# Expert stages: when each half of the next gate and up weights is loaded

## What is computed

```python
def block(args):
    tids, e, w = args
    xb = x_pad[tids]
    hdn = jax.nn.silu(xb @ w1[e]) * (xb @ w3[e])
    return (hdn @ w2[e]) * w[:, None].astype(xb.dtype)
```

## Time and profile before

| what | us |
|---|---|
| median of 3 runs | 3187.47 |
| lowest and highest | 3185.77 to 3190.87 |
| profiled execution, its own time | 3187.16 |
| its span, first to last instruction | 3185.40 |
| busy TensorE | 3063.2 |
| busy VectorE | 2140.7 |
| busy ScalarE | 1584.9 |
| busy GpSimd | 400.5 |

### The profile page before, as it was taken

How to read it: one execution, slowest core, us unless ns; L and a number is a source line. 1 busy time by engine, 2 the same in 40 slices (tenths; PEclk the granted TensorE clock), 3 DMA queues, 4 the chain that set the end, 5 groups by cost and what they waited for, 6 DMA issues and landing times.

```text
span 3185.4 us, 39317 instructions
## 1 busy us (share of the span) xinstructions
PE 3063.2 (96%) x14891; PEld 2373.3 (75%) x14891; DVE 2140.7 (67%) x2334; ACT 1584.9 (50%) x1905; POOL 400.5 (13%) x275
## 2 busy tenths in 40 slices
PE   8999899999999999999999989988999999999998
PEld 7668677777758867677776757877888888788887
DVE  3475788888863375888888865564476646767662
ACT  3573577777753271777777753442322223622211
POOL 0001222222220002222222240010000000000000
PEclk9999899999999998999999999999999999999999
DMA  7303699999972124899998963220223222232322
GB/s 271 113 1 126 261 362 359 349 363 356 353 273 100 37 77 169 327 357 351 344 364 342 357 200 93 53 53 1 93 80 106 93 106 93 86 113 80 106 93 79
DMA packets 174737, 600.47 MB, mean 189 GB/s; under 512 B 25538, under 2 KB 74866, under 8 KB 125204
## 3 DMA queue, kind: packets, MB, share of 16 engines
q1 hardware_dynamic: 140432, 541.22, 46.4%
q0 software_dynamic: 23680, 52.61, 4.6%
q10 hardware_dynamic: 10499, 4.91, 0.6%
HBM read 582.01 MB, written 48.23 MB: 198 GB/s over the span
## 4 chain that ended last, share of the span: by engine, by line
PE 84%; DMA 6%; DVE 4%; ACT 3%; issue 2%; POOL 1%; DVEq 0%; SPq 0%; POOLq 0%; ACTq 0%
PE bank L1948 21%; PE bank L1950 21%; PE bank L1949 21%; PE bank L1960 3%; DMA ring<-w_gate 2%; PE bank L2617 2%; PE bank L2012 1%; PE bank L2013 1%; PE bank L2341 1%; PE bank L1955 1%; DMA expert_rows<-lnp 1%; PE bank L1956 1%; PE bank L2306 1%; PE bank L2112 1%; PE bank L2378 1%
## 5 line engine op out<-in xcount | busy, mean ns | idle before, releaser
L1949 PE MATMUL bank<-ring_rounded,big_rounded 128*96 128x512 f32 (+1 forms) x1768 | 696.0, 394 | 0.0
L3363 DVE TENSOR_TENSOR ring_rounded<-ring,big_rounded 128x2048 fp32r<-128x2048 f32 x252 | 567.2, 2287 | 38.6 <-ACT big_rounded L1389 37.1
L1389 ACT ACTIVATE big_rounded<-ring 128x2048 fp32r<-128x2048 f32 x252 | 478.3, 1918 | 63.3 <-DMA ring<-w_up 53.4
L2916 DVE TENSOR_TENSOR ring_rounded<-ring,ring_rounded 128x2048 fp32r<-128x2048 f32 (+2 forms) x118 | 260.3, 2245 | 334.4 <-ACT ring_rounded L1146 334.1
L1146 ACT ACTIVATE ring_rounded<-ring 128x2048 fp32r<-128x2048 f32 (+2 forms) x124 | 226.7, 1877 | 376.0 <-DMA ring<-ffn_w_down 151.1
L1948 PE MATMUL bank<-big_rounded 128*96 128x512 f32 x992 | 394.7, 398 | 0.4 <-DVE ring_rounded L3363 0.4
L3363 DVE TENSOR_TENSOR ring_rounded<-ring,ring_rounded 128x2048 fp32r<-128x2048 f32 x128 | 292.7, 2288 | 151.3 <-ACT ring_rounded L1389 150.7
L1950 PE MATMUL bank<-big_rounded,XH_rounded 128*96 128x512 f32 x992 | 392.1, 395 | 0.0
L1949 PEld LDWEIGHTS bank<-ring_rounded,big_rounded 128*96 128x96 f32 (+1 forms) x1768 | 294.6, 167 | 109.3
L1389 ACT ACTIVATE ring_rounded<-ring 128x2048 fp32r<-128x2048 f32 x128 | 245.0, 1916 | 223.2 <-DMA ring<-w_gate 222.9
L1948 PE MATMUL bank<-ring_rounded,big_rounded 128*96 128x512 f32 (+1 forms) x776 | 312.3, 403 | 10.7 <-issue 5.1
(11 more groups left out here) (484 smaller groups left out, 5052.9 us busy)
## 6 DMA issues: line engine op xcount, KB each, us to landing
ring<-w_up SPq DMA_DIRECT2D x128, 1024.0 KB, 7.9
ring<-w_down SPq DMA_DIRECT2D x128, 1024.0 KB, 7.9
ring<-w_gate SPq DMA_DIRECT2D x128, 1024.0 KB, 5.5
ring<-ffn_w_up SPq DMA_DIRECT2D x44, 1024.0 KB, 7.5
ring<-ret_gdn_w_in SPq DMA_DIRECT2D x8, 2048.0 KB, 12.8
ring<-ffn_w_down SPq DMA_DIRECT2D x8, 2048.0 KB, 7.8
expert_rows<-lnp POOLq DMA_DIRECT2D x1, 12288.0 KB, 41.9
ring<-odd_w_qkv SPq DMA_DIRECT2D x6, 2048.0 KB, 7.9
```

The lines of the kernel that those rows point to most:

```text
L1389: act.activation(one_pass(expert_hi(j)), expert_raw(j), ACT.Copy).then_inc(signal("half_rounded").sem, 1)
L1949: pe.matmul(dst, x_hi, y_lo, start=False, stop=False)
L2916: dve.tensor_tensor(one_pass(w), w, parts(hi(c)[:, ks, :]), ALU.subtract).then_inc(split[c.pair], 1)
L3363: dve.tensor_tensor(one_pass(expert_raw(j)), expert_raw(j), parts(expert_hi(j)), ALU.subtract).then_inc(signal("half_split").sem, 1)
```

## The change

There is one new signal, `half_used`, in place of `down_half`. TensorE increments it after the fourth of the eight steps of gate and of up, and after the first half of the down products, three times for each expert. SP waits for it before the first half of gate and of up, and issues that half alone; the second half is issued behind `full[2]` or `full[3]`, as before. In the first expert of a layer the increments come after the first four of the products with the remainders. The first down half of the last expert gets the same treatment. `halves_used` counts the increments. A helper with no caller, `keep_busy`, is removed.

```diff
@@ load_experts and beside it
+        def halves_used(l, e):
+
+            return 3 * EXPERTS * l + 1 if isinstance(e, int) and e == 0 else e * 3 + 3 * EXPERTS * l
+
@@
                 def next_gate_up(e):
 
-                    for b, js in ((2, GATE), (3, UP)):
+                    for i, (b, js) in enumerate(((2, GATE), (3, UP))):
+                        sp.wait_ge(signal("half_used").sem, halves_used(l, e) + i)
+                        expert_half(e + 1, js[0])
                         sp.wait_ge(full[b], e + (base[b] + 1))
-                        for j in js:
-                            expert_half(e + 1, j)
+                        expert_half(e + 1, js[1])
 
                 def next_down(e):
 
-                    sp.wait_ge(signal("down_half").sem, e + EXPERTS * l)
+                    sp.wait_ge(signal("half_used").sem, halves_used(l, e) + 2)
                     expert_half(e, DOWN[0])
@@
-                sp.wait_ge(full[2], base[2] + EXPERTS)
                 w = a["w_down"][l][EXPERTS - 1].rearrange("(h p k) n -> h p k n", p=P, h=2)
                 for j in DOWN:
+                    if j == DOWN[0]:
+                        sp.wait_ge(signal("half_used").sem, halves_used(l, EXPERTS - 1))
+                    else:
+                        sp.wait_ge(full[2], base[2] + EXPERTS)
                     sp.dma_start(last_down(expert_raw, j), w[j % 2]).then_inc(half_loaded[j - 4], 16)
@@ up_first
                                 ins = remainder(psum[b][0:CAP, :], M["XET"][:, half, 4 * i + kk, :], expert_raw(j)[:, kk, :], 4 * i + kk == KD - 1)
+                            if i == 0:
+                                ins.then_inc(signal("half_used").sem, 1)
                         ins.then_inc(full[b], 1)
@@ up
                                           expert_hi(j)[:, kk % 4, :], expert_raw(j)[:, kk % 4, :], kk == 0, kk == KD - 1)
+                            if kk == 3:
+                                ins.then_inc(signal("half_used").sem, 1)
                         ins.then_inc(full[b], 1)
@@ down
                         if j == DOWN[0]:
-                            ins.then_inc(signal("down_half").sem, 1)
+                            ins.then_inc(signal("half_used").sem, 1)
```

More of the change, by code:

```diff
@@ L2207, in turn_qk @@
                     ins.then_inc(full[v.bank], 1)
-            def keep_busy(v, n):
-                pe.matmul(ps(v)[:, 0:n], ident, const[:, 0:n], start=True, stop=True)
             def windows():
```

## The result

The changed kernel takes 3163.57 us (median of 6, 3161.89 to 3169.86) against 3185.93 us for the kernel before, measured beside it. The ratio is 0.9929, with a 95% interval of 0.9913 to 0.9944: 22.4 us, 0.7% faster. Later, in another comparison of the same two kernels, it was 3164.99 and 0.9929 (0.9911 to 0.9947).

The account below looks back on a forecast made before the run. TensorE, 96% busy, was taken as the bound, losing time when the first gate half lands late. Terms 18 + 1.0 + 2.5 = 21.5, say 22 us, gave 3187.2 - 22 = 3165 us, range 3159 to 3176 (8 in 10).

Parts of the forecast that it names:

- The late stages: Full expert stages of both layers: up to all 19.8 us of excess over 18.08 us stages can go; 18 us taken.
- the same chain: Late stages: first gate half lands, ScalarE rounds, VectorE makes remainder, then hidden product; transposes wait, losing 0.70 us a stage.
- VectorE's earlier work: Stage without loss: this, not the load, comes next once the gate half is early, hiding landings up to 2 us later.
- no up load stands in the chain: Late stages: the first gate half's landing sets TensorE's loss; no down or up load is in that chain.
- the 2.8 us of the prediction: Expert stages: the first gate half is issued 12 x 0.24, about 2.8 us, earlier.
- landing bound by the queue: Rival, 9%: first gate half waits behind up and down halves, landing moves half as much; gain 12, 3175 us.
- The bandwidth rival: Rival, 4%: stage loads capped at 357 or 358 GB/s; smoothing brings only 1.5 + 6.0 us, 3178 us.
- The slower rival: Rival, 6%: early gate half delays the second down half up to 2.5 us, holding up ScalarE; 3205 us.
- The first stages: First expert of each layer: an earlier load start cuts TensorE's idle time before hidden transposes; 1.0 us for both layers.
- The last stages: First layer's last down products: splitting the down pair saves 0.8 us idle and 1.7 us half speed; 2.5 us.
- that the half-speed stretch goes with the longer idle time: First layer's last down products: half-speed stretch taken, as a choice, to go with the idle time; 1.7 us.
- Signals and waits: Two more increments and two more SP waits per expert: zero cost, at most 1 us over 62 stages.

Follow-up runs that it names:

- gate half alone: Changed kernel with only the first gate half loaded early; up halves and last down halves wait as in the kernel before: 3168.71 us, ratio 0.9937.
- gate half later: Against the kernel before, both gate halves are issued together only after four of the eight up steps: 3296.77 us, ratio 1.0358.
- reordered kernel: Kernel before, loads untouched; ScalarE and VectorE take row copies, remainders and the product of hidden ahead of the first gate half: 3178.62 us, ratio 0.9975.
- early up half alone: Changed kernel with only the first up half loaded early; both gate halves stay behind the last gate product: 3180.20 us, ratio 0.9978.
- output rows earlier: Kernel before, loads untouched; ScalarE copies a stage's output rows ahead of rounding the first up half: 3194.97 us, ratio 1.0021.
- gate products first: Changed kernel with X scaled before VectorE's first stage, and each layer's first expert finishing gate, remainders included, before up: 3158.49 us, ratio 0.9911.

## Why the prediction was right, point by point

The forecast of 3165 us held, and so did the sum: 21.5 us predicted, 17.4 + 2.3 + 3.0 - 1.0 = 21.7 found at the places of the change, 22.4 between the medians, in which the wait at 93 us and the other places outside the experts may have a part. That the parts agree to 0.2 us with the sum is luck in some measure: three of its terms were off, both ways. Term by term:

**The late stages: 18 predicted, 17.4 measured.** The kernel with the gate half alone, the one with the gate half later and the reordered kernel meet at the same chain from three sides, so this step is shown. One more late stage stood outside the 58: the second layer's last one, 17.72 us before and 17.13 after, so the term is 18.0 in all. The working put the end of `hidden` 3.0 us ahead of the transposes, and it is 818.62 against 821.66; but what comes last there is not VectorE's earlier work, as the working said. VectorE still waits 0.29 us for ScalarE, and ScalarE 0.66 us for the gate load, since the landing moved by 1.6 us only. The number met for another reason. And the sentence that no up load stands in the chain may be too strong: with the early up half alone fewer landings of the gate half were late. The five late stages that are left stand mostly near the starts of the layers. The gate loads issued at 389.8 and 392.6 us took about 10 us to land. A row store of 13.0 us on GpSimd had ended at 382.9, with a gather behind it and another store and gather at 387.9 and 389.2; but the gate loads issued at 371.7, during that long store, took 5.3 us, so it is not shown to be the cause.

**The landing moved less than the issue, and it cost nothing.** Counted from the hidden transposes, the first gate half was issued at 690.52 - 684.17 = 6.35 us in the even stage before (its transposes start 18.08 us ahead of 702.25), and is at 807.15 - 803.58 = 3.57 now: the 2.8 us of the prediction. But its rounding moved only from 695.97 - 684.17 = 11.80 us to 813.78 - 803.58 = 10.20, by 1.6 us, and over all stages the median landing went from 12.4 to 10.8. The missing part is the longer flight, 7.3 us against 5.6. So the rival "landing bound by the queue" was right about the landing and wrong about its price. It paid half the gain for half the movement; but a late stage loses only 0.7 us, so a landing 1.6 us sooner, with the spread of the landings as it is (the latest 14.7 us after the transposes before, 13.6 after), clears nearly all of them. A gain that hangs on a threshold must not be priced in proportion.

**The bandwidth rival fell.** Over 525 us the loads ran at 361 and 362 GB/s, both above what a ceiling of 357 or 358 would allow, and the stages gained 17.4 and not 7.5 us. The Trainium skill's figure of about 358 GB/s for each NeuronCore ("DMA: Bandwidth & Descriptors", Specifications) doesn't bind here. Its page "HBM Reference", Specifications (TRN2), says that it is the share with both cores of a pair streaming, and that a core alone gets more; this kernel on one core agrees with that.

**The slower rival fell at its condition.** It needed the second down half to be rounded 3.2 us later than before. It is rounded 7.62 us after the hidden transposes, against 7.74; the down loads' median time to landing even fell, from 7.8 to 7.2 us in the first layer.

**The first stages: 1.0 predicted, 2.3 measured, 1.5 in the second trace.** The idle time shrank by 0.91 and 1.12 us, as worked out (0.97); in the second trace by 1.05 and not at all. The half-speed stretch also shortened, from 10.2 to 6.8 us, which the prediction had named as the upper end of 1.9 us and more. The shorter idle time is not shown to be the reason: with the up half alone the stretch is 6.8 us in both layers as well, and the idle time 7.06 and 7.02 us. Against that a wait grew that it had not named: VectorE comes late to the first down half, 0.99 us where it was 0.36, because its scaling of X stands ahead and the rest has moved up.

**The last stages: 2.5 predicted for one layer, 2.4 measured there, of which 1.0 was lost again** while the rows return. The split, 0.8 of idle time and 1.7 of half speed, fits this layer; but that the half-speed stretch goes with the longer idle time was a choice, and the other traces don't bear it out. The 0.6 us of the second layer are the late stage named above, and not this place.

**Signals and waits: nothing, and nothing was seen:** a stage without loss takes 18.08 us with them as without.

**What stays open.** Why the early up half alone leaves fewer late landings of the gate half. How the longer flight of the gate half divides between its neighbours in the queue and the row traffic. What decides over the wait at 93 us, over the time behind the last row store, and over where the half-speed stretches fall. And whether the parts beyond the gate half are worth anything in the total.

## What to carry to other kernels

When a load can only be issued as its place comes free, signal each part of the place at its own end, and first for the part whose landing stands ahead of dependent work in another engine's fixed order. Read the slack in a stage that has no loss: it tells how far the landing must move, and a change that moves it a little further gains all there is, with any further move worth nothing. Ask at the same time whether the order itself can be turned, since here it alone gave 15.5 of the 19.8 us in the stages; but look at the first pass of the loop, where the same order meets other work.

## What the runs showed of the hardware

**A load that has company takes longer, and not by little.** The 1 MB gate loads land 5.6 us after issue in the median of the first layer when sent as a pair into a queue that is running dry (in the last half microsecond before the issue the weight loads keep the DMA engines 34% busy, in the median of the 58 stages), and 7.3 us when sent one at a time, close behind the down load (100% busy). In the kernel with the output rows earlier, the same load takes 4.8 to 5.0 us where GpSimd's gather starts after its landing, and 6.54 us on average where the gather starts within 5.0 us of the hidden transposes. The Trainium skill says, in "DMA: Bandwidth & Descriptors", Queues, rings and completion order, that each DMA engine takes turns between queues by packets. That would let small row transfers hold up a large load; the flights agree with it, but no run here isolates it.

**One idle gap does not tell how long the clock stays low.** Ahead of the first stages' hidden transposes TensorE idled 7.07 and 7.12 us before, with 10.2 us at half speed; 6.16 and 6.00 us after, with 6.8; and 3.99 and 2.39 us with the gate products first, with 3.4. That looks like a rule, but other traces break it: 7.06 and 7.02 us with the up half alone and 7.25 in the second trace of the changed kernel went with 6.8 us, and 5.99 us with the gate half alone went with 10.2. The row with the up half alone, first layer:

```profile
344.20:351.00 6.80, 4.06 (x12) 2.75 (x13) 6.10 (x6) 4.45 (x4) 0.00 (x0) 0.50 0.82 288
```

So shorter half-speed stretches came along with the change in both layers, but a saved idle microsecond can't be counted on to bring them.
